# Weight splits moved behind the normalisation work, and one projection moved behind the gate sums, in a three-layer fp32 network kernel

## The reference, cut to what matters

```python
for i in range(2):
    h = h + 0.5 * swiglu(rmsnorm(h, norm_ffn1[i]), gate1[i], up1[i], down1[i])
    h = h + mixer_i(rmsnorm(h, norm_mix[i]))            # dilated / neighbourhood attention
    h = h + 0.5 * swiglu(rmsnorm(h, norm_ffn2[i]), gate2[i], up2[i], down2[i])
    gate = sigmoid(rmsnorm(h, norm_ple[i]) @ w_ple_gate[i])
    h = h + gate * (p[i] @ w_ple_proj[i])
x = rmsnorm(h, norm_final)
# third layer
proj = rms_norm(x, norm_mix) @ w_in                     # RWKV, pooling, attention and gate columns
y_a = ((yn + bonus) * g)                                # g = sigmoid(gd) @ g2, the "gate sums"
y_b = multiscale_pool(p_pool)                           # four groups, windows 2, 4, 8, 16
y_c = gqa_axial(p_att)
x = x + merged(y_a, y_b, y_c) @ w_out
x = x + expert_choice_ffn(rms_norm(x, norm_ffn), ...)   # 16 experts
out = rms_norm(x, norm_final_2)
```

## Time and profile before

| | |
|---|---|
| median of 3 runs | 3425.86 us |
| the profiled execution's own time | 3423.94 us |
| its span in the trace | 3422.6 us |
| TensorE (PE) busy | 3274.6 us (96%) |
| VectorE (DVE) busy | 1553.1 us (45%) |
| ScalarE (ACT) busy | 1079.0 us (32%) |
| GpSimd (POOL) busy | 295.0 us (9%) |
| mean granted TensorE clock | 0.992 |
| DMA, mean over the span | 130 GB/s |

### The profile page before, as it was taken

How to read it: one execution, slowest core, us unless ns; L and a number is a source line. 1 busy time by engine, 2 the same in 40 slices (tenths; PEclk the granted TensorE clock), 3 DMA queues, 4 the chain that set the end, 5 groups by cost and what they waited for, 6 DMA issues and landing times. The chain is left out here.

```text
span 3422.6 us, 47184 instructions
## 1 busy us (share of the span) xinstructions
PE 3274.6 (96%) x20498; PEld 2493.5 (73%) x20498; DVE 1553.1 (45%) x2214; ACT 1079.0 (32%) x1580; POOL 295.0 (9%) x345
## 2 busy tenths in 40 slices
PE   8999999999999999999999999969999999988887
PEld 7888777888888888888688888748876887433223
DVE  5443556544436444333744434685467544211103
ACT  4222226432224322223632223543344324100001
POOL 1000131200001000000210000211011301000000
PEclk9999999999999999999999999989999999999999
DMA  3223321122233222332222222301010224699997
GB/s 140 99 87 102 117 87 38 38 99 93 86 97 113 99 93 85 104 125 75 75 87 99 99 85 95 110 19 48 4 63 20 102 97 159 259 423 421 427 425 316
DMA packets 58957, 445.62 MB, mean 130 GB/s; under 512 B 7424, under 2 KB 9088, under 8 KB 28800
## 3 DMA queue, kind: packets, MB, share of 16 engines
q1 hardware_dynamic: 58752, 442.61, 34.4%
HBM read 440.49 MB, written 2.10 MB: 129 GB/s over the span
## 5 line engine op out<-in xcount | busy, mean ns | idle before, releaser
L540 DVE TENSOR_TENSOR w_lo<-slot,w_hi 128x2048 fp32r<-128x2048 f32 (+4 forms) x243 | 487.0, 2004 | 340.8 <-ACT w_hi L531 339.2
L165 PE MATMUL bank<-xa,w_hi 128*128 128x512 f32 x1368 | 543.4, 397 | 13.4 <-DVE xa L583 9.9
L166 PE MATMUL bank<-xa,w_hi 128*128 128x512 f32 x1368 | 533.3, 390 | 0.0
L167 PE MATMUL bank<-xa,w_lo 128*128 128x512 f32 x1368 | 533.0, 390 | 0.0
L531 ACT ACTIVATE w_hi<-slot 128x2048 fp32r<-128x2048 f32 (+4 forms) x243 | 405.9, 1670 | 356.6 <-PE bank L167 349.9
L165 PE MATMUL bank<-xb,w_hi 128*128 128x512 f32 x832 | 324.6, 390 | 0.0
L166 PE MATMUL bank<-xb,w_hi 128*128 128x512 f32 x832 | 323.7, 389 | 0.0
L167 PE MATMUL bank<-xb,w_lo 128*128 128x512 f32 x832 | 323.7, 389 | 0.0
L165 PEld LDWEIGHTS bank<-xa,w_hi 128*128 128x128 f32 x1368 | 257.2, 188 | 77.0 <-issue 23.2
L166 PEld LDWEIGHTS bank<-xa,w_hi 128*128 128x128 f32 x1368 | 257.2, 188 | 57.7 <-issue 5.5
L167 PEld LDWEIGHTS bank<-xa,w_lo 128*128 128x128 f32 x1368 | 257.2, 188 | 53.9
(11 more groups left out here) (477 smaller groups left out, 4945.2 us busy)
## 6 DMA issues: line engine op xcount, KB each, us to landing
slot<-in_w_gu SPq DMA_DIRECT2D x87, 1024.0 KB, 4.7
slot<-in_exp_gate SPq DMA_DIRECT2D x25, 2048.0 KB, 12.1
slot<-in_exp_up SPq DMA_DIRECT2D x24, 2048.0 KB, 15.9
slot<-in_exp_down SPq DMA_DIRECT2D x24, 2048.0 KB, 15.8
slot<-in_w_dn SPq DMA_DIRECT2D x64, 704.0 KB, 4.1
slot<-in_w_gate SPq DMA_DIRECT2D x24, 768.0 KB, 4.3
xe<-in_exp_up SPq DMA_DIRECT2D x8, 2048.0 KB, 15.2
xe<-in_exp_down SPq DMA_DIRECT2D x8, 2048.0 KB, 15.9
```

The lines of the kernel that those rows point to most:

```text
L165: e.matmul(out, w[0], x[0], start=(j == 0), stop=False)
L166: e.matmul(out, w[0], x[1], start=False, stop=False)
L167: return e.matmul(out, w[1], x[0], start=False, stop=(j == n - 1))
L540: dve.e.tensor_tensor(lo, slot(k, b), hi.bitcast(F32), ALU.subtract).then_inc(L.up("w_lo", b))
```

## The change

Three places change; no instruction is added or removed, only the order on the engines.

In the first FFN the split of block 2 moves from step 0 (ahead of the root) to step 1 (behind the whole of step 0), on ScalarE and VectorE. In both PLEs the split of block i+2 moves from the middle of step i (in step 0 from behind the root) to the head of step i+1, on both engines. On TensorE the pooling projection 2 moves from ahead of the four gate sums to behind them.

```diff
 def act_ffn                                  # dve_ffn alike, with dve_weight
     for m in range(FF):
-        if f or m != 1:
-            act_weight(k, b0 + m + (1 if f or m else 2))
+        if f or m:
+            act_weight(k, b0 + m + 1)
         if m == 0:
             act_root(k, nm, k.rstd_last)
 def act_ple
-    act_weight(k, b0 + 1)
     for i in range(KT):
+        act_weight(k, b0 + i + 1)
         if i == 0:
             act_root(k, nm, k.rstd_last)
-            act_weight(k, b0 + 2)
         act.wait_ge(*L.at("ple_scaled", layer, i))
         e.activation(m.sgs[i % 2], m.sgs[i % 2], ACT.Sigmoid).then_inc(L.up("ple_sigmoid", layer, i))
-        if 0 < i < KT - 1:
-            act_weight(k, b0 + i + 2)
 def dve_ple
-    dve_weight(k, b0 + 1)
     for i in range(KT):
+        dve_weight(k, b0 + i + 1)
         if i == 0:
             dve_root(k, nm)
-            dve_weight(k, b0 + 2)
...
         e.tensor_tensor(k.h[i], k.h[i], g, ALU.add).then_inc(L.up("h", nx, i))
-        if 0 < i < KT - 1:
-            dve_weight(k, b0 + i + 2)
 def pe_post
         spread("qk_spread", i, k.key_spread if i == 4 else k.head_spread, x.root, ("roped", "ax", i))
-    pe_pool_proj(k, 2)
     b = k.first["g2_pool"]
...
     for j in range(4):
         bank = bank_for(("g_sum", j), ("rwkv_out", j))
         e.matmul(bank[:, :], tok(gw, j), m.lora[2], start=True, stop=True).then_inc(L.up("g_sum", j))
+    pe_pool_proj(k, 2)
```

More of the change, by code:

```diff
@@ L662, in dve_ffn @@
     for m in range(FF):
-        if f or m != 1:
-            dve_weight(k, b0 + m + (1 if f or m else 2))
+        if f or m:
+            dve_weight(k, b0 + m + 1)
         if m == 0:
```

## The result

The changed kernel takes 3456.4 us (median of 4 runs, 3455.8 to 3457.4), the kernel before 3425.9 beside it (3423.9 to 3426.5, 4 runs). The ratio is 1.009, with a 95% interval of 1.0073 to 1.0108: 30.4 us slower. The forecast was 3453.0, in a range of 3443 to 3459.

The account below looks back on a forecast made before the run. TensorE was taken to set the time in the first FFN and PLEs. Terms 7.4 + 4.7 + 10.6 + 6.1 = 28.8 us on the profiled 3423.94 gave 3452.7; the median was put at 3453, range 3443 to 3459.

Parts of the forecast that it names:

- first FFN: wait and clock: First FFN: TensorE waits 5.9 us for block 2's late split, plus 1.5 at low clock: 7.4 us (5.9 to 7.5).
- first PLE: wait, clock, last split: First PLE: one TensorE wait 2.8 us, low clock 1.6, wider last split 0.3: 4.7 us (2.8 to 5).
- second PLE: Second PLE: the loop through ScalarE and VectorE, not TensorE, sets the pace; 10.6 us (8.0 to 12).
- behind the recurrence: Gate sums: TensorE waits 6.4 us for bank 1 instead of 1.6; 4.7 plus 1.4 clock, 6.1 us (4.6 to 6.5).
- The ring: Second PLE: scale, sigmoid, product, sum, copy, split, next scale take 7.8 us a turn, above TensorE's 6.80 a block.
- GpSimd's part: Second PLE: GpSimd's sums of squares hold up VectorE's split, making a turn 7.8 us instead of 7.3.
- The clock: Behind TensorE's long waits: 3.4 us at 1.2 GHz, 8 matmuls instead of 15, costing up to 1.6 us each.
- The two rows on the clock: Kernel before: clock fell to 0.52 after a 2.27 us wait, stayed 1.00 after 3.04; length alone does not decide.
- Rival 1: All four places: waits come, but no clock fall and no GpSimd hold on VectorE; 21.7 us, 3446; chance 0.22.
- Rival 2: FFN and PLEs: two buffers hide the splits, only the projection's move counts; 6.1 us, 3430; chance 0.05.
- Rival 4: Expert stage: weight stream starts at its old time and swallows the shift, not slower; 3424 to 3426; chance 0.04.
- rival 3: Second PLE slowed by GpSimd's whole sums, plus new low-clock stretches in attention and merge; 35.6 us, 3459; chance 0.10.

Follow-up runs that it names:

- the first four experiments: One part of the change each against the kernel before: first FFN 3431.9 us, first PLE 3431.7, second PLE 3439.3, pooling projection 2's move 3432.7.

## Why the prediction was right, step by step

| step | forecast, us | profile after | alone |
|---|---|---|---|
| first FFN: wait and clock | 5.9 + 1.5 = 7.4 | 5.9 + 2.9 = 8.8 | 8.0 |
| first PLE: wait, clock, last split | 2.8 + 1.6 + 0.3 = 4.7 | 3.0 + 1.6 + 0.5 = 5.1 | 5.1 |
| second PLE | 10.6 | 11.3 | 11.3 |
| behind the recurrence | 4.7 + 1.4 = 6.1 | 4.6 + 2.3 = 6.9 | 4.6 + 2.9 = 7.5 |
| sum | 28.8 | 32.1 | 31.9 |

- **The waits** were right to 0.1 or 0.2 us in the first FFN, behind the recurrence and in the first PLE. They came from dates on the engines that make the block, not from the length of what was moved: neither of the two costs of a split (1.9 and 2.3) is 5.7.
- **The ring** of the second PLE was right in kind and in size: a turn of 7.9 against the forecast's 7.8, the split 2.09 against 2.0, the waits of TensorE of 3.45, then 0.8, then 1.64 in the order that was named. The 0.7 us that are missing are 5 turns by 0.1, and 0.2 at the first scale, which was put where the split had started. It comes 0.2 later: the scale reads what the reciprocal writes and starts 0.1 us after its end, where the split had started 0.1 before it.
- **GpSimd's part** was an inference from two rows; shortening the sums has shown it.
- **The clock** is the step that was mis-sized. It was priced as if each stretch were the one of the earlier trace rows, 1.5 us. It cost 2.1 to 2.9 in the first FFN and 2.3 to 2.9 behind the recurrence; in the first PLE it cost the 1.6 that was forecast. A stretch priced from one other stretch is a guess about its length: the one in the earlier trace rows held 8 slow matmuls, the two in the first FFN held 10 and 14.
- **The two rows on the clock** The earlier trace rows are each one execution. In the run with the first FFN alone both are the other way round, behind the same waits of 3.04 and 2.27 us. The first of these rows answers to 2510.10 in the earlier trace rows, the second to 2853.30:

```profile
2518.66:2522.06 3.40, 3.40 (x39) 0.74 0.82 313
2862.46:2865.86 3.40, 3.40 (x15) 1.00 0.79 254
```

The first costs 1.6 us and the second saves as much. Among the ten profiles, five have the low stretch behind the 3.04 us wait and six have it behind the 2.27 us wait. So the forecast was right to say that the length of a wait doesn't settle it. It read more than that out of the two rows, that the 2.27 us wait was followed by it because it stood among full matmuls, and this is not borne out.

- **Rival 1** (no extras) is out: both extras were there, and taking them away left about its terms (5.8 for 5.9, 4.6 for 4.7; 8.9 for 8.0, where one whole sum, 0.65 us, had been left in). **Rival 2** is out with the first wait. **Rival 4** is out: the expert stream's waits are 23.7 against 24.4, and the stream did start as much later as TensorE, 33.0 us, as its first loads show, before and after:

```profile
2859.67 40.09 SPq L521 DMA_DIRECT2D slot<-in_exp_gate  x4
2892.66 40.09 SPq L521 DMA_DIRECT2D slot<-in_exp_gate  x4
```

Of **rival 3** one piece was seen, stretches at the lower clock where there were none before: 1.6 us near 657. Its other piece, the whole sum on each split, was not.

- **The sum.** The profiled execution was put at 3452.7 and took 3458.0. Of these 5.3 us, 3.3 are the four places (32.1 for 28.8): 2.3 the clock, 0.7 the second PLE, the rest the first PLE. The other 2.0 lie outside them: 1.6 near 657, 1.1 in the expert stage, less 0.7 at the start. The median is nearer, 3456.4 for 3453. It rose by 30.4, 1.6 more than the sum, and the forecast had counted the sum from an execution 1.9 us below the median of before. That 28.8 comes so near to 30.4 is in part luck, since the sum of the places in the trace is 32.1.
- One reading of the waits was too broad. The table of before has a wait of TensorE over 2 us in the first FFN: 9.9 us at the very start, for the first input (`xa`). It stands ahead of all four places and enters no term.

That a piece of rival 3 turns up in code that is the same in both kernels has a plainer reading than a consequence of the change. The same place in the kernel with only the projection moved, where all that comes before it is as in the kernel before: first its wait and the clock behind it, then the kernel before at the same distance from that wait (1.41 us).

```profile
650.49 0.47 PE L165 MATMUL bank<-xa,w_hi 128*128 128x512 f32 x1 [1.88 <-POOL xa L888]
...
651.90:655.10 3.20, 3.20 (x9) 0.50 0.28 44
```

```profile
648.51 0.47 PE L165 MATMUL bank<-xa,w_hi 128*128 128x512 f32 x1 [1.88 <-POOL xa L888]
...
649.92:653.12 3.20, 3.20 (x15) 1.00 0.34 51
```

Same code, same wait of 1.88, one with 9 matmuls in 3.2 us and one with 15. The low stretch costs 1.6 us here. Six of the ten profiles have it, four don't. So a low stretch can come or stay away behind one and the same wait. By this place (0 or 1.6 us) and the one behind the recurrence's wait (0 or 2.0) alone two executions can differ by 3.6 us without a cause in the code, and a scatter of this size is what the whole runs have: the kernel before ran between 3421.2 and 3427.8 us beside the first four experiments. What decides it from one execution to the next stays open; no run here was made to tell.

## What to carry to other kernels

When a step that makes something ahead of need is moved behind the step that uses it, write down the loop as a ring (scale, sigmoid, product, sum, copy, split, next scale) and compare its turn with the block of the engine that bounds: below it, the move costs one wait, above it the difference in every turn. When independent work is moved out from between two uses of one PSUM bank, the price is the cover that it gave, since the engine that frees the bank does not come earlier. And where a whole run scatters by 0.1%, measure an edit of a few microseconds as the distance between two fixed instructions around it, and keep the clock behind each wait as a term of its own with both ends.

## What the hardware showed that was not expected

- A wait of 5.66 and one of 5.68 us at the same place of the same stage were followed by 10 and by 14 matmuls at the lower clock, 2.1 and 2.9 us of loss. A wait of 3.45 us in the second PLE was followed by the lower clock in one profile (0.61 over 4 us) and not in another (1.00).
- A wait of 1.88 us in the attention stage was followed by a low stretch of 1.6 us of loss in six profiles and not in four, and the small matmuls behind the 27.8 us wait took 8.1 to 8.5 us or 10.1 to 10.3, with the same instructions and waits around them.
- Useless matmuls in a wait that can't be avoided kept the clock up in the one profile of each and made the place 2.2 us (first FFN) and 2.9 us (gate sums) cheaper in the trace; the time of the whole run did not fall by an amount that could be measured.
